# Heads of the two mixers: VectorE reads the gate rows first, ScalarE's residual copies later, the sixth low half behind the sixth convolution, the ninth convolution behind K*beta

## The reference

```python
def l2norm(x):
    return x * lax.rsqrt(jnp.sum(x * x, -1, keepdims=True) + NORM_EPS)

def token_mixer(h, w_in, w_out, gdn_conv, gdn_a_log, gdn_dt_bias, gdn_norm, ...):
    qkv_a, a_a, b_a, z_a, qkv_b, qk_c, v_c, i_c, f_c, o_c = jnp.split(h @ w_in, IN_SPLITS, axis=-1)
    qa, ka, va = jnp.split(causal_conv_silu(qkv_a, gdn_conv), 3, axis=-1)
    qa = l2norm(split_heads(qa).astype(f32))
    ka = l2norm(split_heads(ka).astype(f32))
    va = split_heads(va).astype(f32)
    g = -jnp.exp(gdn_a_log.astype(f32)) * jax.nn.softplus((a_a + gdn_dt_bias).astype(f32))
    beta = jax.nn.sigmoid(b_a.astype(f32))
    oa = gated_delta_rule(qa, ka, va, g.transpose(0, 2, 1), beta.transpose(0, 2, 1)).transpose(0, 2, 1, 3)
    ...
```

## Time and profile before

| | us |
|---|---|
| median of 3 runs | 1775.43 (1773.72 to 1776.09) |
| the profiled execution, its own time | 1776.33 |
| its span | 1774.3 |
| mean granted TensorE clock | 0.988 of 2.4 GHz |
| second mixer's head behind the first's | 614.16 |

### The profile page before, as it was taken

One profiled execution on the slowest core, in us unless ns is written; L12 is line 12 of the kernel. 1 busy time (PEld: TensorE's weight loads), 2 busy tenths in 40 slices (PEclk: granted clock), 3 DMA queues, 4 the chain that ended last, 5 costly groups with the idle time before them and its releaser, 6 DMA issues. The chain is left out here.

```text
span 1774.3 us, 30736 instructions
## 1 busy us (share of the span) xinstructions
PE 1686.1 (95%) x13112; PEld 1512.1 (85%) x13112; DVE 1323.5 (75%) x1965; ACT 777.0 (44%) x997; POOL 6.3 (0%) x14
## 2 busy tenths in 40 slices
PE   2999989999999999999899999999999999999998
PEld 2999978888899989999798779999886555759898
DVE  7777788855877778998878557999767768567844
ACT  2433365323633354343753327343652345355354
POOL 0000000000000000000000000000000000000000
PEclk9999999999999999999999999999999999999999
DMA  9868536351577746885364435776153200223102
GB/s 390 340 270 305 207 108 246 133 202 63 203 305 285 282 180 271 321 316 198 119 227 155 179 128 207 273 279 229 48 213 143 95 34 15 107 95 143 48 24 96
DMA packets 48807, 331.92 MB, mean 187 GB/s; under 512 B 5256, under 2 KB 8480, under 8 KB 9376
## 3 DMA queue, kind: packets, MB, share of 16 engines
q1 hardware_dynamic: 47808, 326.79, 48.2%
q0 software_dynamic: 864, 3.17, 0.7%
HBM read 328.87 MB, written 1.07 MB: 186 GB/s over the span
## 5 line engine op out<-in xcount | busy, mean ns | idle before, releaser
L347 PE MATMUL ps<-xhi,low 128*128 128x256 f32 x2048 | 499.5, 283 | 4.2 <-ACT xhi L1459 4.2
L347 PEld LDWEIGHTS ps<-xhi,low 128*128 128x128 f32 x2048 | 360.5, 190 | 6.4 <-ACT xhi L1459 5.6
L347 PE MATMUL ps<-xhi,whi_wk 128*128 128x256 f32 x1072 | 298.5, 288 | 40.5 <-ACT xhi L1459 38.7
L347 PE MATMUL ps<-xlo,whi_wk 128*128 128x256 f32 x1072 | 291.5, 281 | 0.0
L1459 ACT ACTIVATE wk<-ps 128x256 f32<-128x256 f32 (+5 forms) x219 | 108.1, 503 | 386.8 <-PE ps L347 320.8
L1459 ACT ACTIVATE whi_wk<-ring 128x2048 fp32r<-128x2048 f32 x100 | 191.6, 1918 | 195.3 <-DMA ring<-in_stream_dram 145.2
L347 PEld LDWEIGHTS ps<-xhi,whi_wk 128*128 128x128 f32 x1072 | 203.5, 195 | 43.2 <-issue 41.8
L2068 DVE TENSOR_TENSOR low<-ring,whi_wk 128x2048 fp32r<-128x2048 f32 (+1 forms) x101 | 228.4, 2264 | 6.6 <-ACT whi_wk L1459 6.6
L347 PE MATMUL ps<-wk 64*64 64x64 f32 (+10 forms) x2712 | 210.3, 262 | 5.8 <-ACT wk L1459 4.3
L347 PEld LDWEIGHTS ps<-wk 64*64 64x64 f32 (+4 forms) x2712 | 162.3, 146 | 55.0 <-issue 29.5
L347 PEld LDWEIGHTS ps<-xlo,whi_wk 128*128 128x128 f32 x1072 | 197.9, 189 | 0.0
(11 more groups left out here) (141 smaller groups left out, 2861.7 us busy)
## 6 DMA issues: line engine op xcount, KB each, us to landing
ring<-in_stream_dram SPq DMA_DIRECT2D x302, 1024.0 KB, 5.7
ring<-in_cond_dram SPq DMA_DIRECT2D x4, 1024.0 KB, 4.6
wk<-spread_dram POOLq DMA_DIRECT2D x4, 384.0 KB, 5.1
wk<-spread_dram POOLq DMA_DIRECT2D x2, 768.0 KB, 6.9
tab<-in_tab_dram SPq DMA_DIRECT2D x1, 1440.0 KB, 20.5
res<-in_xt_dram SPq DMA_DIRECT2D x1, 1024.0 KB, 17.5
res<-in_ct_dram SPq DMA_DIRECT2D x1, 1024.0 KB, 9.9
out_dram<-wk SPq DMA_DIRECT2D x4, 256.0 KB, 2.4
```

What stands on the lines that cost most here:

```text
L347: last[0] = nc.tensor.matmul(o, l, r, start=start, stop=stop, skip_group_check=free)
```

## The change

- VectorE: the end of `norm` no longer waits for "normed" ahead of a mixer; the first read of bank 1 no longer waits for ScalarE's read of it. `r_u`, `r_ab` and `r_ln` move to other memory, so that the copies still find `ff_cen`.
- ScalarE: the eight residual copies become `normed(m, part)`, two times four, issued in the mixer behind high halves 5 and 6; behind an ffn's norm they stay where they were. The sigmoid of the output gate goes behind high half 4 and waits for VectorE's read. `fill(1)`, `fill(1)` and high half 8 are mixed with the silus 6 to 8.
- VectorE: low half 5 goes from between the fourth and the fifth convolution to behind the sixth, ahead of `rows()`. The ninth convolution (tile 8) goes behind K*beta, and low half 7 thus comes directly behind the eighth.
- TensorE: the same instructions in the same order, other waits. "kk" waits for K*beta ("kbk") alone, no more for V*beta and the mask; "qk" waits for the reads of banks 4 to 6 instead of the exponentials ("ekd"); "pairs" waits for no bank reads; "l2" also for the sigmoid.

```diff
--- before.py
+++ after.py
@@ -227,7 +227,7 @@
         r_cs, r_rw, r_max, r_nm, r_beta = [W(ROWS + 256 * i, 256) for i in range(5)]
         colt = tiles(W(COLT, 256), 128)
         g_t, g_tt, g_dt, g_at, g_att = [W(SCR + 1536 * i, 1536) for i in range(5)]
-        r_u, r_ab, r_ln = [g_at[:, 256 * i:256 * i + 256] for i in range(3)]
+        r_u, r_ab, r_ln = W(23040, 256), W(23296, 256), r_rw
         g_sq = g_t
         g_pair = g_att
         g_t, g_tp = g_t[:, 0:768], g_t[:, 768:1536]
@@ -648,6 +648,7 @@
                     if i == 4:
                         for p in range(3):
                             eng.wait_ge(*step_of("proj_read", m, p))
+                        eng.wait_ge(scalar_done, step("proj_read_a", m, 0))
                         eng.wait_ge(scalar_done, step("l2sq", m))
                         for t in range(6):
                             mm(banks(1, 1536)[:, 256 * t:256 * t + 256], blk, tiles(g_sq, 256)[:, t], True, True)
@@ -656,16 +657,13 @@
                 fill(2)
 
                 eng.wait_ge(vector_done, step("rows", m))
-                for p in range(3, 6):
-                    eng.wait_ge(*step_of("proj_read", m, p))
                 eng.wait_ge(scalar_done, step("l2e", m))
                 for t in range(2):
                     turn(bank(1, P * t, P * t + P), r_rw[:, P * t:P * t + P])
                 last[0].then_inc(tensor_done, 1)
                 done.named("pairs", m)
                 fill(2)
-                eng.wait_ge(vector_done, step("kb", m))
-                eng.wait_ge(vector_done, step("gb_read", m))
+                eng.wait_ge(vector_done, step("kbk", m))
 
                 K, Q = qkv[:, 3:6], qkv[:, 0:3]
                 for h in [0, 2, 4, 1, 3, 5]:
@@ -676,7 +674,9 @@
                         mm(banks(1, 1536)[:, P * u:P * u + P], head(K, h, c), head(g_kb, h, c), True, True)
                 last[0].then_inc(tensor_done, 1)
                 done.named("kk", m)
-                eng.wait_ge(scalar_done, step("ekd", m))
+                for p in range(3, 6):
+                    eng.wait_ge(*step_of("proj_read", m, p))
+                eng.wait_ge(scalar_done, step("proj_read_a", m, 5))
                 for h in [0, 2, 4, 1, 3, 5]:
                     if h == 1:
                         row_tile(1)
@@ -1582,10 +1582,17 @@
                         whole(m + 1, c)
                     else:
                         win_high(m + 1, c)
+                if to_ffn:
+                    normed(m, 0)
+                    normed(m, 1)
+
+            def normed(m, part):
+
                 g0_, b0_ = COLS["ln_g"][0] + 8 * m, COLS["ln_b"][0] + 8 * m
-                affine(m, res[:, :, XS], tiles(ff_cen, 256), cols[:, g0_:g0_ + 8], cols[:, b0_:b0_ + 8], range(0, 4))
-                eng.wait_ge(vector_done, step("xn", m, 3))
-                affine(m, res[:, :, XS], tiles(ff_cen, 256), cols[:, g0_:g0_ + 8], cols[:, b0_:b0_ + 8], range(4, 8), "normed", m)
+                if part:
+                    eng.wait_ge(vector_done, step("xn", m, 3))
+                affine(m, res[:, :, XS], tiles(ff_cen, 256), cols[:, g0_:g0_ + 8], cols[:, b0_:b0_ + 8], range(4 * part, 4 * part + 4),
+                       *(("normed", m) if part else ()))
 
             def ffn(l, f):
                 m = 3 * l + 2 * f
@@ -1684,8 +1691,6 @@
                         part(s)
                     at["n"] += n
 
-                eng.wait_ge(tensor_done, step("proj", m, 0))
-                gate_or_copy(24, bank(1, 0, 256), "proj_read_a", m, 0)
                 eng.wait_ge(vector_done, step("rab", m))
                 act(r_ln, r_ab, ACT.Exp, scale=-1.0).then_inc(scalar_done, 1)
                 eng.wait_ge(scalar_done, done.count)
@@ -1694,12 +1699,13 @@
                 eng.wait_ge(scalar_done, done.count)
                 act(r_ln, r_ln, ACT.Ln, "rln", m, bias=1.0).then_inc(scalar_done, 1)
                 win_high(m, 4)
+                eng.wait_ge(vector_done, step("proj_read", m, 0))
+                gate_or_copy(24, bank(1, 0, 256), "proj_read_a", m, 0)
                 for t in range(6):
                     silu(t)
-                    if t == 1:
-                        win_high(m, 5)
-                    if t == 3:
-                        win_high(m, 6)
+                    if t in (1, 3):
+                        win_high(m, 5 + t // 2)
+                        normed(m - 1, t // 2)
                 eng.wait_ge(scalar_done, done.count)
                 act(g_sq, W(QKV, 1536), ACT.Square, "l2sq", m).then_inc(scalar_done, 1)
                 one_table()
@@ -1709,13 +1715,14 @@
                 win_high(m, 7)
                 eng.wait_ge(tensor_done, step("proj", m, 5))
                 gate_or_copy(9, bank(6, 256, 512), "proj_read_a", m, 5)
+                fill(1)
                 silu(6)
                 silu(7)
+                fill(1)
+                win_high(m, 8)
                 silu(8)
-                win_high(m, 8)
-                fill(2)
                 eng.wait_ge(pairs_in, 32 * (l + 1))
-                eng.wait_ge(vector_done, step("kb", m))
+                eng.wait_ge(vector_done, step("kbk", m))
                 cs = tiles(g_pair[:, 768:1536], 256)
                 act(g_eg, cs[:, :, P:T], ACT.Exp, "eg", m).then_inc(scalar_done, 1)
                 for t in range(3):
@@ -2261,7 +2268,8 @@
                     affine(res[:, :, XS], cen, col("ln_g", 40, 8), col("ln_b", 40, 8), range(4, 8))
                     eng.wait_ge(vector_done, done.count)
                     tt(sq_x[:, 4:8], res[:, 4:8, XS], res[:, 4:8, XS], MUL, "sqx", 1).then_inc(vector_done, 1)
-                eng.wait_ge(scalar_done, step("normed", m))
+                if m % 3:
+                    eng.wait_ge(scalar_done, step("normed", m))
 
             def ffn(l, f):
                 m = 3 * l + 2 * f
@@ -2421,10 +2429,8 @@
 
                 if l == 0:
                     eng.wait_ge(tables_in, 16)
-                for i, ch in enumerate(WIN_FIRST):
+                for i, ch in enumerate(WIN_FIRST[:5]):
                     eng.wait_ge(tensor_done, step("proj", m, i))
-                    if ch in (12, 4):
-                        eng.wait_ge(scalar_done, step("proj_read_a", m, i))
                     if ch == 12:
                         ts(r_u, bank(1, 256, 512), col("row_bias", l), ADD, col("row_sign"), MUL, "proj_read", m, i).then_inc(vector_done, 1)
                         eng.wait_ge(vector_done, done.count)
@@ -2432,11 +2438,12 @@
                         stt(r_ab, r_u, -1.0, r_u, MUL, ALU.max, "rab", m).then_inc(vector_done, 1)
                         win_low(m, 3)
                         continue
-                    for t in ((2 * ch, 2 * ch + 1) if ch < 4 else (8,)):
-                        conv(t, bank(1 + i, 256 * (t % 2), 256 * (t % 2) + 256), *(("proj_read", m, i) if t % 2 or t == 8 else ()))
-                    if ch < 2:
-                        win_low(m, 4 + ch)
+                    for t in (2 * ch, 2 * ch + 1):
+                        conv(t, bank(1 + i, 256 * (t % 2), 256 * (t % 2) + 256), *(("proj_read", m, i) if t % 2 else ()))
+                    if ch == 0:
+                        win_low(m, 4)
                     if ch == 2:
+                        win_low(m, 5)
                         rows()
                         win_low(m, 6)
 
@@ -2449,7 +2456,9 @@
                 copy(W(COLT, 256), bank(1, 0, 256), "colt", m).then_inc(vector_done, 1)
                 eng.wait_ge(pairs_in, 32 * (l + 1))
                 copy(glast, tiles(g_pair[:, 768:1536], 256)[:, :, P - 1], "glast", m).then_inc(vector_done, 1)
-                tt(g_kb, qkv[:, 3:6], tiles(g_pair[:, 0:768], 256), MUL).then_inc(vector_done, 1)
+                tt(g_kb, qkv[:, 3:6], tiles(g_pair[:, 0:768], 256), MUL, "kbk", m).then_inc(vector_done, 1)
+                eng.wait_ge(scalar_done, step("proj_read_a", m, 5))
+                conv(8, bank(6, 0, 256), "proj_read", m, 5)
                 eng.wait_ge(scalar_done, step("silu", m, 8))
                 tt(g_vb, qkv[:, 6:9], tiles(g_pair[:, 0:768], 256), MUL, "kb", m).then_inc(vector_done, 1)
                 fill(3)
```

## The result

The changed kernel takes **1777.16 us** (median of 20 runs, 1774.37 to 1782.03); the kernel before, timed beside it, takes 1774.51 us (20 runs, 1771.92 to 1776.48). The ratio is **1.0014, interval 1.0007 to 1.002**: by the 0.2% that tells a difference it is the same, and if anything 2.5 us slower. 1766.0 was forecast, with 1761.0 to 1771.0 as the range, so the result lies outside it.

The account below looks back on a forecast made before the run. TensorE, busy 1686.1 of 1774.3 us, was taken as the bound, with a 5.24 us gap and half-clock sums in each mixer's head. Two mixers at 4.7 us give 9.4 us: 1766.0 us, range 1761.0 to 1771.0.

Parts of the forecast that it names:

- The gate read: VectorE's read of the gate rows in the first mixer: starts at 243.1 without its 3.64 us wait for ScalarE.
- the sums: Twelve matmul records summing squares of Q and K: start at 264.7 instead of 269.32, gap 0.6 instead of 5.24 us.
- low half 6: VectorE's step behind the gate recurrences in the first mixer: ends at 274.1, TensorE waits 0.8 us.
- low half 7: VectorE's step behind convolutions 6 and 7 in the first mixer: ends at 280.6, TensorE waits 0.6 us.
- the transposes: TensorE's 64x64 transposes in the first mixer: reached at 298.7.
- The sum: Gain over both mixers, 2 x 4.7 = 9.4 us, giving 1766.0 us on the median; chance 0.62.
- Rival 4: Nothing changes, because another release stood just behind ScalarE's at 246.76: 1775.4 us; chance 0.05.
- rival 5: VectorE keeps up better than forecast in the mixers: 1761.4 us; chance 0.08.
- rival 2: Broadcast of beta and decay lands behind two 1 MB loads, 2.2 us late for K*beta: 1770.4 us; chance 0.07.
- the forecast need: The time, 282.8, at which K*beta in the first mixer needs the broadcast of beta and decay.
- rival 3: Broadcast behind the next two loads too, at 291.4; beyond 287.5 a mixer is slower than before: 1783.2 us; chance 0.03.
- Rival 1: Clock falls all the same at the short gap before the sums, gain 4.0 per mixer: 1767.4 us; chance 0.10.

Follow-up runs that it names:

- experiment 4: Changed kernel, but SP's queue sends both DMAs of the beta and decay broadcast ahead of the two 1 MB loads: 1765.49 us, ratio 0.994 to the kernel before.
- experiment 1: Changed kernel, but SP waits for the broadcast of beta and decay before sending the two 1 MB loads: 1768.44 us, ratio 0.9948 to the kernel before.
- experiment 3: Changed kernel with five matmuls of no use between the transposes and kk's wait for K*beta: 1775.20 us, ratio 0.999 to the kernel before.
- experiment 2: Changed kernel with only the second of the two 1 MB loads held back for the broadcast of beta and decay: 1768.30 us, ratio 0.9956 to the kernel before.
- experiment 10: Kernel of experiment 4, but POOL sends the decays only when the pairs (beta and summed decay) have landed: 1778.37 us, ratio 1.0016 to the kernel before.
- experiment 7: Kernel of experiment 4 with low half 5 back between the fourth and fifth convolution: 1772.59 us, ratio 0.997 to the kernel before.
- experiment 8: Kernel of experiment 4 with the ninth convolution back ahead of low half 7 and the old waits for kk and qk: 1772.85 us, ratio 0.9973.

## Why the prediction was wrong

**Right, to a few tenths.** The gate read without a wait (243.22; 243.1 forecast), the sums (264.88; 264.7) behind 0.61 us (0.6) at the full clock, low half 6 done at 271.79 + 2.29 = 274.08 (274.1), low half 7 at 280.5 (280.6), and with the pairs in time the transposes at 298.66 (298.7). The sum, 9.4 us, is what the change is worth when nothing is in the pairs' way: experiment 4's ratio is a gain of 8.2 to 13.0 us of 1775.43, experiment 1's of 6.7 to 11.9. Rival 4 (nothing changes) and rival 5 are out.

**The step that failed** is the one in rival 2 and behind the sum: "It landed 7.9 us after the recurrences' end", and so "now 279.6: 3.2 us to spare". Of the 7.9, 5.1 us is the landing of a broadcast that no load preceded. It is also the median of two DMAs counted from the issue of the first. The second was sent 0.7 us later and took 5.7, so both were there 9.2 us after the recurrences' end, and even by the old landing 1.3 of the 3.2 us to spare were not there. The text named the two loads that would now go first, priced them at the longest landing seen, 9.6 us, got 285.0 and gave it a chance of 0.07. The pairs were sent from 274.59 on and were there at 287.7, 4.9 us after the forecast need (282.8), of which 2.7 are beyond that bound. Both sizes in it were too small. The two loads of after, sent at 273.18 and 273.56, took:

```profile
ring<-in_stream_dram SPq DMA_DIRECT2D x1, 1024.0 KB, 5.6
ring<-in_stream_dram SPq DMA_DIRECT2D x1, 1024.0 KB, 10.8
```

So the second took 10.8 us, not 9.6, and landed at 284.4, not 283.0. And the pairs came 3.3 us behind it, not the "2 us for its own 0.77 MB". These came from the rate of weight loads, 410 GB/s; the windows have 197 to 225 from 281 to 285.

**The point of rival 3 was right, its chance was not.** It said that a landing at 287.5 makes the mixer as slow as before. With the rows: from VectorE's small copy to the next projection's start it is 10.23 us in experiment 1 (281.46 to 291.69), and the same in experiment 3, in its second mixer (900.27 to 910.50), and 5.63 more to the transposes (291.69 to 297.32). From after's 287.70 that gives 303.56; the kernel before has 303.37, and after's list runs 0.18 us later here (its norm's sums start 0.19 later, at 228.95 against 228.76). **By this working the wait alone takes the whole 4.7 us of a mixer's gain and no more.** The prediction let the next projection hang on low half 8, and that fits: in experiments 1 to 3 it starts 0.14 to 0.15 us behind the end of low half 8 (289.26 + 2.29 = 291.55 in experiment 1, start 291.69). The profile names ScalarE, but its copy out of PSUM there runs from 291.49 to 291.85 and ends after that start.

**The clock does the rest.** Rival 1 looked for a fall at the gap before the sums, where there is none. It came at the gap before kk, which exists only by the late pairs. The transposes stand at 306.33 instead of 303.56, 2.77 us later. In the second mixer it is 923.80 - 904.85 = 18.95 us from the small copy to the transposes, where 10.23 + 5.63 = 15.86 would do: 3.09 more. Together that is 5.9 us, and the two profiled executions differ by 5.70. The median run loses 2.5 to 2.7. That its pairs land sooner, as those of experiment 3 did (9.4 us), would explain it; only one execution of after was profiled, so this is argued, not shown. (The cold spell of before was a little shorter than the prediction has it: with 0.83 granted in the microsecond from 267 it began near 267.7, so it lasted 6.8 us and not 7.2. Only rival 1 uses that.)

**The Trainium skill against the runs.** The forecast let the sum stand by the Trainium skill, "DMA: Bandwidth & Descriptors", section "Queues, rings and completion order", by which an engine changes between its queues packet by packet. After's trace agrees with it in part. The second load landed at 284.4, just ahead of the first of the pairs (274.59 + 10.1 = 284.7), which is what sharing looks like. But from 276 to 279, with the pairs already sent, the engines move 377 to 434 GB/s, the rate of loads, and the low rate comes only from 279 on (279 GB/s, then 283, then 197 to 225), when the first load has landed (273.18 + 5.6 = 278.8). In experiment 1, with no load ahead, the low rate is there within 2 us of the issue (238 GB/s from 275, sent at 273.25). How much of this is order and how much sharing is not settled. The inference from the rule failed in either case: with 2 MB gone first, a broadcast of 0.77 MB was not on time. Of the Trainium skill's "TensorE: Matmul & The Clock Gate", section "A second HAM failure mode: psum-queue depth-cycling", by which frequent small idle times make the clock swing, nothing is seen in the mixers' heads of experiments 1 and 4: with gaps of 0.61, 0.78, 0.36 and 0.64 to 0.96 us in a row the granted clock stays at 1.00.

## What to carry to other kernels

When an edit lets TensorE run ahead, list the transfers that its releases now start earlier, and ask which small transfer on the critical chain they will overtake: a landing time from the old trace holds only for what was in flight beside it. A deadline transfer belongs ahead of the bulk loads in the issuing order (here six lines turned "no gain" into 0.6%), and the next one in the same chain must not pay for it (experiment 10 gave the whole gain back). And price a wait of a microsecond or two on TensorE together with the clock behind it, at the place where it falls.

## What was not expected of the hardware

- The two DMAs of the pairs are dear for their bytes, the broadcast of the decays is not. The first window below is experiment 10's, with only the loads behind the pairs in flight beside them; the second is experiment 7's, with the decays alone in flight. The engines are as busy and move 216 against 406 GB/s. By the code each DMA of the pairs goes to 64 partitions in rows of 1 KB, that of the decays to all 128 in runs of 6 KB; that this makes the difference was not tried.

```profile
276.00:277.00 1.00, 1.00 (x11) 1.00 (x10) 0.96 (x3) 0.63 (x3) 0.00 (x0) 1.00 1.13 216
276.00:277.00 1.00, 1.00 (x11) 1.00 (x10) 0.93 (x3) 1.00 (x1) 0.00 (x0) 1.00 1.00 406
```

- The clock's answer to a gap is not a matter of the gap's length alone. After 0.96 us (experiment 4, second mixer), 2.12 (experiment 7, second) and even 2.53 (experiment 8, first) it stayed at 1.00; after 0.97 us (experiment 3, first mixer) it fell. The windows of the last:

```profile
293.00:294.00 1.00, 0.10 (x1) 0.00 (x0) 0.93 (x1) 1.00 (x5) 0.00 (x0) 1.00 1.02 426
294.00:295.00 1.00, 0.92 (x5) 0.95 (x6) 0.94 (x1) 0.24 (x1) 0.00 (x0) 0.61 0.76 311
```

- How long the clock stays low differs much from place to place. Behind after's 2.26 us, with kk and qk (64 rows) following, it was low from 288 to 302; in experiment 2, behind 1.82 us with a projection following, from 293 to 297. What makes the difference (the gap, or the work behind it) was not tried.
